# A decoder trunk's sparse-attention stage: two blocks of ties settled later, prompt jobs a slot deeper, row tiles scaled and rotated by GpSimd, loads reordered

## The reference

```
def _odd_layer(x, pos, mk, mv, attend, norm_g, w_in, qn, kn, w_out, mem_qn):
    xn = _rms(x, norm_g)
    q, k, v, g_c, qi, wi, ki, xq, g_x = _split(xn @ w_in, ODD_SPLITS)
    q = _rope(_rms(heads(q, AT_HEADS), qn), pos)      # 8 heads of 128
    k = _rope(_rms(heads(k, AT_KV_HEADS), kn), pos)   # 2 heads of 128
    yC = attend(q, k, v, qi, wi, ki).reshape(B, T, AT_W) * jax.nn.silu(g_c)
    y = jnp.concatenate([yC, yX.astype(yC.dtype)], axis=-1) @ w_out
    return x + y.astype(x.dtype), (k, v, ki)

def _index_select(qi, wi, ki, qpos, topk):
    s = ...                                           # indexer scores, -inf above the diagonal
    _, idx = lax.top_k(s, topk)                       # of equal scores the first ones
    return idx, idx <= qpos[None, :, None]

def _sparse_attend(q, kg, vg, valid):
    s = jnp.where(valid, einsum(q, kg) * Dh ** -0.5, -jnp.inf)
    return einsum(softmax(s), vg)
```

## Time and profile before

| what | value |
| --- | --- |
| median of 3 runs | 2043.4 us (2040.61 to 2052.66) |
| the profiled execution | 2048.12 us, of it the profile's span 2046.1 us |
| TensorE matmul busy | 1854.9 us, 91% |
| VectorE / ScalarE / GpSimd busy | 989.0 (48%) / 595.6 (29%) / 398.4 us (19%) |
| mean granted TensorE clock | 0.958 of full |
| back stage | 1576.7 to 2046.1, of it output products from 1886.0 |

### The profile page before, as it was taken

How to read it: one execution, slowest core, us unless ns; L and a number is a source line. 1 busy time by engine, 2 the same in 40 slices (tenths; PEclk the granted TensorE clock), 3 DMA queues, 4 the chain that set the end, 5 groups by cost and what they waited for, 6 DMA issues and landing times. The chain is left out here.

```text
span 2046.1 us, 26819 instructions
## 1 busy us (share of the span) xinstructions
PE 1854.9 (91%) x9553; PEld 1423.8 (70%) x9553; DVE 989.0 (48%) x2326; ACT 595.6 (29%) x1261; POOL 398.4 (19%) x639
## 2 busy tenths in 40 slices
PE   4999999999998997998999898999887897888998
PEld 3766788777787776886875466777665564666887
DVE  4522543224565645213431667778776555575211
ACT  1111332111111103101211347676534343444000
POOL 4201221000132342000331002211005515120000
PEclk9999999999899998998999998999988889899999
DMA  5334333544244547222122112324424834223221
GB/s 177 118 120 123 96 110 99 160 152 144 83 162 138 145 155 272 83 91 86 52 70 64 43 63 83 100 92 160 132 75 122 266 100 145 85 83 99 100 94 57
DMA packets 126950, 235.14 MB, mean 115 GB/s; under 512 B 28354, under 2 KB 52322, under 8 KB 126818
## 3 DMA queue, kind: packets, MB, share of 16 engines
q1 hardware_dynamic: 106706, 168.53, 25.5%
q0 software_dynamic: 18912, 60.57, 9.3%
q10 hardware_dynamic: 1200, 4.33, 0.5%
HBM read 167.22 MB, written 66.16 MB: 114 GB/s over the span
## 5 line engine op out<-in xcount | busy, mean ns | idle before, releaser
L1160 PE MATMUL layer_acc<-layer_w_hi,layer_xT_hi 128*128 128x512 f32 x640 | 266.2, 416 | 0.2 <-PE all_banks L1305 0.2
L1162 PE MATMUL layer_acc<-layer_w_hi,layer_xT_lo 128*128 128x512 f32 x640 | 256.5, 401 | 0.0
L1161 PE MATMUL layer_acc<-layer_w_lo,layer_xT_hi 128*128 128x512 f32 x640 | 256.3, 401 | 0.0
L2650 PE MATMUL front_acc<-front_w_hi,front_xT_hi 128*128 128x512 f32 x520 | 221.1, 425 | 15.9 <-DVE front_st L3104 8.2
L2652 PE MATMUL front_acc<-front_w_hi,front_xT_lo 128*128 128x512 f32 x520 | 208.3, 401 | 0.0
L2651 PE MATMUL front_acc<-front_w_lo,front_xT_hi 128*128 128x512 f32 x520 | 208.0, 400 | 0.0
L1160 PEld LDWEIGHTS layer_acc<-layer_w_hi,layer_xT_hi 128*128 128x128 f32 x640 | 124.4, 194 | 31.5 <-issue 6.1
L1161 PEld LDWEIGHTS layer_acc<-layer_w_lo,layer_xT_hi 128*128 128x128 f32 x640 | 123.7, 193 | 27.3 <-issue 2.6
L1162 PEld LDWEIGHTS layer_acc<-layer_w_hi,layer_xT_lo 128*128 128x128 f32 x640 | 123.2, 192 | 27.9
L2650 PEld LDWEIGHTS front_acc<-front_w_hi,front_xT_hi 128*128 128x128 f32 x520 | 100.3, 193 | 48.9 <-DVE front_st L3104 10.7
L2962 ACT ACTIVATE front_index_rows<-odd_bias,front_candidate 128x1024 bf16<-128x1024 f32 (+3 forms) x128 | 124.8, 982 | 6.9 <-DVEq L3285 5.0
(11 more groups left out here) (639 smaller groups left out, 3690.9 us busy)
## 6 DMA issues: line engine op xcount, KB each, us to landing
all_w<-in_w_even POOLq DMA_DIRECT2D x80, 256.0 KB, 3.9
h_even<-layer_st SPq DMA_DIRECT2D x79, 256.0 KB, 2.1
all_w<-in_w_odd POOLq DMA_DIRECT2D x61, 256.0 KB, 3.6
h_odd<-front_st SPq DMA_DIRECT2D x56, 256.0 KB, 2.0
layer_scratch<-h_even SPq DMA_DIRECT2D x51, 256.0 KB, 3.1
all_scratch<-in_w_mem SPq DMA_DIRECT2D x32, 256.0 KB, 3.7
back_first_smp<-in_cache_attn_v POOLq DMA_DIRECT2D x64, 128.0 KB, 3.2
all_scratch<-h_even SPq DMA_DIRECT2D x28, 256.0 KB, 3.7
```

The costliest lines, as they stand in the source:

```text
L1160: T.matmul(out[0:rows, :], xh[:, kk, to], wh[:, r, :], start=(kk == 0), stop=False)
L1161: T.matmul(out[0:rows, :], xh[:, kk, to], wl[:, r, :], start=False, stop=False)
L1162: ins = T.matmul(out[0:rows, :], xl[:, kk, to], wh[:, r, :], start=False, stop=(kk == KC - 1))
L2650: T.matmul(out[0:rows, :], xh[:, k, to], wh[:, r, :], start=(k == 0), stop=False, skip_group_check=True)
```

## The change

1. **Ties.** Blocks 5 and 4 leave the front stage; new streams `late_ties` (VectorE, slots 3, 5, 7, 9 of the back stage) and `late_biases` (ScalarE, slots 5 and 9) settle them, and job 32 waits for them. `find` is stepped once a slot in slots 62 to 71 (13 steps stood in 11 slots before), and `qk` starts at slot 62 instead of 63, with the transposes of its two tiles in two slots.
2. **Jobs.** The steps of a job are spread over four slots: mix of g-3, transposes of g-2, scores of g; three buffers `sm`, three `neg`, four `tot`. The plan has 77 slots.
3. **Row tiles.** `prep` starts at 8p-14. GpSimd now raises, multiplies by the root (L3769), by gamma (L3773) and rotates, each linked to the one before; VectorE keeps only the sums.
4. **Value pages.** GpSimd loads those of sequences 4 and 6, SyncE those of 5 and 7. SyncE loads row tile 2 ahead of the key pages of unit 3.
5. **Weights.** GpSimd starts the first four slices in slot 39, once the sample keys have been transposed; VectorE waits for the stored sample result instead.

```diff
-    for s, n in zip(range(62, 73), (2, 1, 1, 1, 2, 1, 1, 1, 2, 1, 1)):
-        plan[s] += ["find"] * n
+    for s in range(62, 72):
+        plan[s].append("find")
...
-    for s in range(63, 73):
+    for s in range(62, 73):
         plan[s].append("qk")
...
+    NOW = len(BY_DVE) + 1 + len(BY_ACT) - len(LATE_TIES)
...
-                todo = [(COL[i], P, rows_at(i)) for i in BY_DVE] + [(LAST, SMP, smp)] + [(COL[i], P, rows_at(i)) for i in BY_ACT]
+                todo = [(COL[i], P, rows_at(i)) for i in BY_DVE] + [(LAST, SMP, smp)] + [(COL[i], P, rows_at(i)) for i in BY_ACT if i not in LATE_TIES]
...
-            dve.wait_ge(nsd, NC)
+            dve.wait_ge(nsd, NOW)
...
+LATE_TIES = (5, 4)
...
-    for g in range(66):
+    for g in range(67):
         plan[g].append("job")
-    for s in range(41, 65):
+    for s in (3, 5, 7, 9):
+        plan[s].append("ties")
+    for s in range(39, 65):
         plan[s].append("weights")
-    for s in range(65, 76):
+    for s in range(66, 77):
         plan[s].append("out")
...
-    STEPS = [[(p, s - (8 * p - 15)) for p in range(2, T1) if 0 <= s - (8 * p - 15) < 6] for s in range(57)]
+    STEPS = [[(p, s - (8 * p - 14)) for p in range(2, T1) if 0 <= s - (8 * p - 14) < 6] for s in range(57)]
...
                 load_k(2)
+                load_qk(2)
                 load_k(3)
-                load_qk(2)
                 load_qk(3)
...
                         if step == 0:
                             pool.wait_ge(red, p - 1)
-                            G.tensor_tensor(ssq[u][0:rows, :], ssq[u][0:rows, :], c.half[0:rows, 0:H10], ALU.pow).then_inc(rsd, 1)
+                            link(G.tensor_tensor(ssq[u][0:rows, :], ssq[u][0:rows, :], c.half[0:rows, 0:H10], ALU.pow))
+                            link(G.tensor_tensor(y, y, bc(ssq[u][0:rows, :], 2, HD), ALU.mult))
                         if step == 1:
...
+                            for lo, hi, j, n in ((0, QH * HD, 0, QH), (QH * HD, QK, 1, KVH)):
+                                part = heads(qk[u][0:rows, lo:hi], n)
+                                link(G.tensor_tensor(part, part, bc(gam[0:rows, j, :], 1, n), ALU.mult))
+                        if step == 2:
+                            rotate(G, link, y, HD // 8, rt[:, PREP[p]], tmp, rows, H10)
+                            pool.sem_inc(rq, 1)
...
-                    if w in (4, 5, 8, 9):
-                        load_v(VRING + 2 * (w // 4 - 1) + w % 2, range(PAGES))
+                    if w in (4, 8):
+                        load_v(VRING + w // 4 - 1 + (w == 8), range(PAGES))
...
             def weights():
-                pool.wait_ge(sst, 16 * 2 * 4)
+                pool.wait_ge(ktr, 2 * (UNITS - 2))
...
-                    if g >= 2:
-                        mix(g - 2)
-                    if 1 <= g <= JOBS:
-                        transposes(g - 1)
+                    if g >= 3:
+                        mix(g - 3)
+                    if 2 <= g < JOBS + 2:
+                        transposes(g - 2)
                     if g < JOBS:
                         scores(g)
...
-                        if step == 1:
-                            dve.wait_ge(rsd, p - 1)
-                            V.tensor_tensor(y, y, bc(ssq[u][0:rows, :], 2, HD), ALU.mult).then_inc(scd, 1)
-                        if step == 2:
-                            dve.wait_ge(gd, 2 * (p - 1))
-                            rotate(V, link2, y, HD // 8, rt[:, t], tmp, rows, H10)
-                            dve.sem_inc(rq, 1)
...
+            def late_ties():
+                for i in LATE_TIES:
+                    j, w, v = 7 - i, P * (i + 1), c.bias[:, bias_at(i):bias_at(i + 1)]
+                    e, m, at = eq[:, 0:w], cum[:, 0:w], c.lowest[:, j:j + 1]
+                    link(V.tensor_scalar(e, v, at, 0.0, ALU.is_equal, ALU.add, accum_out=ties[:, :]))
+                    link(V.tensor_tensor_scan(m, e, e, 0.0, ALU.add, ALU.max))
+                    yield
...
```

More of the change, by code:

```diff
@@ L3475, in rotate @@
     link(eng.tensor_tensor(x2, t[2], t[3], ALU.add))
+LATE_TIES = (5, 4)
 def back_plan():
[L3480 removed]
+    plan = [[] for _ in range(77)]
     for s in range(1, 39):
@@ L3989, in outputs @@
                     yield
-            follow(plan, 0, None, prep=preps(), smp=smps(), job=jobs(), weights=idle(), out=outputs())
+            follow(plan, 0, None, prep=preps(), smp=smps(), job=jobs(), ties=idle(), weights=idle(), out=outputs())
         @block.scalar
```

128 lines of the change are left out of this document (81 added, 47 removed).

## The result

The changed kernel takes 2051.45 us, median of 20 runs, beside 2043.47 us for 20 runs of the kernel before: ratio 1.0037, 95% interval 1.0024 to 1.0050. It is 8 us slower by the medians, under the 1% that one measurement tells apart, but clear over so many runs.

What follows compares the result with a forecast made beforehand. TensorE was taken to bound the kernel, with row tile chains deciding its stalls. Terms -7.0, +15.2, -1.4 and +1.9 made +8.7 us on the median 2043.4, so 2052; bounds and the two near rivals reach 2027 and 2070.

Steps and rivals of the forecast that it cites:

- front stage: Front stage's end: without the ties of blocks 5 and 4 it comes 7.0 us earlier, between 3 and 10.
- back stage to slot 13: Back stage's start: GpSimd's 36 pages and two row tiles hold TensorE, +12.2 us, plus 3 for its clock: +15.2.
- slots 14 to 63: Back stage's later row tiles: windows of chain plus TensorE work, row tile 5 at +5.9, others mostly shorter: -1.4 us.
- end: After the last scores: one more slot of mixing and its reciprocal before the first output product, 6.0 becomes 8: +1.9 us.
- Late ties at nothing: Back stage slots 3 to 9: VectorE's some 9 us of ties lie under its waiting, so cost nothing; at most 9.
- Deeper jobs at nothing: Back stage slots: spreading jobs over more slots has little to win by itself; row tile chains decide.
- GpSimd's chain: Back stage row tiles: the chain takes 16.5 us, 18.5 with loads and contention, longer than its three slots in every block.
- clock term of +3: Back stage to slot 13: after a stall of about 10 us, some 3 us of TensorE work take twice their time.
- Weights and SyncE's pages at nothing: Back stage: SyncE's value pages and weights begun in slot 39 cost nothing, DMA being busy 0.2 to 0.5.
- contention rival: Back stage row tiles: contention stretches GpSimd's work, 2.3 us at each of seven tiles, giving 2068 us; chance 0.21.
- hidden chain: Back stage: ScalarE and GpSimd are ready long before TensorE, so the stalls go, giving 2007 us; chance 0.10.
- pages that run ahead: Back stage: GpSimd prepares pages while its tensor work runs, 20 of 36 save 0.6 us, giving 2033; chance 0.15.

Runs made afterwards that it cites:

- Experiment 1: Kernel before, with only the ties of blocks 5 and 4 moved into the back stage and the front's new plan: 2041.42 us, ratio 0.9979.
- version 10: Changed kernel, root product and rotation on VectorE, sequence 4's pages a slot later, ties back in the front stage: 2012.81 us, ratio 0.9851 to the kernel before.
- 8: Changed kernel, with root product and rotation back on VectorE and sequence 4's value pages a slot later: 2004.03 us, ratio 0.9821 to the kernel before.
- experiment 2: Kernel before, with only the jobs a slot deeper and three score buffers: 2025.73 us, ratio 0.9911.
- Experiment 7: Changed kernel, each row tile begun a slot earlier with its transposes left in place: 2033.36 us, ratio 0.9946 to the kernel before.
- experiment 3: Kernel before, with only the product with the root and the rotation moved to GpSimd, each linked: 2081.82 us, ratio 1.0191.
- experiment 4: Changed kernel, with the product with the root and the rotation back on VectorE: 2010.98 us, ratio 0.9829 to the kernel before.
- Experiment 5: Changed kernel, GpSimd's waits for its root and gamma products put off to where the result is used: 2037.9 us, ratio 0.9966 to the kernel before.
- experiment 6: Changed kernel, GpSimd's eight value pages of sequence 4 two slots later, behind row tile 5's rotation: 2047.47 us, ratio 1.0014 to the kernel before.

## Why the prediction came out, point by point

The time forecast was 2052, the measured one 2051.45. Stage by stage the terms are near too; but two parts of the change were priced far from their size, with opposite signs, and that these two errors are of one size was luck. The terms:

| term | forecast | in the profile |
| --- | --- | --- |
| front stage | -7.0 | -7.0 |
| back stage to slot 13 | +15.2 | +17.7 |
| slots 14 to 63 | -1.4 | -6.5 |
| end | +1.9 | +3.2 |
| sum | +8.7 | +7.4 |

**Front: right, by its own steps.** TensorE's waits of 1.44 and 1.29 went, the last product ended 2.8 us earlier in the stage (2.3 forecast), and the ties no longer held its end. Experiment 1 shows it alone (7.2).

**Late ties at nothing: wrong.** The step took VectorE's busy share (11.3 of 31.3 us) for cover. Experiment 1 showed 4.9 us of cost, 1.72 of it at a copy that TensorE waits for. In the changed kernel it can't be told from the rest; in version 10 against 8 it is 3.0.

**Deeper jobs at nothing: the largest error.** The prediction read 4.5 us of work in 5.1 of time in the earlier trace rows and then said that depth has little to win by itself. It never multiplied the 0.6 by the slots. In experiment 2 the whole back stage was 16.9 us shorter, ratio 0.9911; a slot of block 7 is 0.75 us shorter (in the changed kernel one of block 5 0.8). The formula for the windows hid the error: it took TensorE's busy time times clock for the new kernel, which leaves out just those waits, and the window's own length for the old one. So part of the gain was in the sum (-2.5, -4.1 and -1.0 in the last windows) without a name, while the text called it nothing.

**GpSimd's chain: the right mechanism, too small.** The prediction said that the chain of a row tile doesn't fit three slots, and that holds. From its squares to its transposes the chain took 13.9, 17.6 and 17.6 us at tiles 6 to 8, where 16.5 was forecast (18.5 without the 2 us ahead of the squares), and 1719.13 - 1695.24 = 23.9 at tile 5, where 23.7 was. The waits were 3.33, 5.73 and 6.11 at tiles 6 to 8, expected 3 to 5, and 14.42 at tile 5, expected about 10; tile 4, expected to wait too, did not. Experiment 7 shows that a slot more takes 2 to 6 us off each part from slot 18 on.

But the price of the move by itself was 39 us (experiment 3) and 42 when undone (experiment 4, 1.0037 to 0.9829), where my terms for it came to 22 (the expectation of experiment 3). Three things are in the difference. First, those 22 took 12 us for the start from the recorded sum, and that sum had already set off the earlier load of row tile 2 against GpSimd's work: GpSimd's wait for the first sums is 9.22 us in experiment 3 and 2.94 in the changed kernel, so 6.3 us of the 17 are an error of the 22 and not of the prediction. Second, the immediate waits. The prediction took 1.15 us for each page; behind a waited-for product three pages took 4.07 to 4.37 us and not 3.45, 3.1 us more in the four gaps. In the kernel before, pages behind GpSimd's work were issued at some 0.55 each, since their numbers had been read while it ran. I had this in a row (four issues in 2.25 us) and used it only for a rival. Experiment 5 shows the whole of it, some 2.4 us lost in each gap and 14 us in the time. Against it, the product over 1280 columns took 2.33 us and not 2.95; the 2.95 was scaled by columns from another product, so that it is twice VectorE's 1.49 showed nothing, and the measured ratio is 1.6. Third, the later parts: in experiment 3 slots 26-33 are 9.1 us longer, 42-49 3.4 and 50-63 5.0, where the terms had 6 at row tile 5 and 1 or less for the others. In the changed kernel itself GpSimd was through with its second tile 77.8 us into the stage, forecast 74.1. One wait of about 10 us was expected at the first or second tile; there were two, 7.29 and 10.46. The clock term of +3 is near: in the 4 us from 1598 the granted clock was 0.55 and in the 5 us from 1641 it was 0.50, which costs some 2 us at each (an estimate: half of the time at half clock).

One row was read for more than it says. The prediction put the 3.26 us at 1776.12 among the stalls around row tiles and held it to be no longer due with the weights of slot 39 in place. The transposes of row tiles waited 1.4 us in all before, so the chain did not decide then; and the same place in the changed kernel, slot 43, still shows most of it:

```profile
1775.84 2.90 PE L3958 MATMUL all_banks<-back_v,back_first_scratch 128*128 128x128 f32 x12 [2.36 <-issue]
```

**Value pages.** That SyncE takes half of them and that the eight of slot 27 lengthen tile 5's chain was right; experiment 6 took 10 us of that wait away. What their place is worth in the time is 3 to 5 us, not the 9 that I expected of experiment 6, because the pages then come late for the value products: two needs for one queue.

**Weights and SyncE's pages at nothing: open, and probably wrong.** Experiment 4's kernel is 34.9 us faster than before by its ratio, and the jobs (18.2) and ties (4.3) by themselves give 22.5. Some 12 us are left for the weights begun in slot 39, SyncE's value pages, the first row tile loaded sooner, the start at 8p-14, and for what these parts give only together. About half may be at the start: up to slot 13 it took 62.8 us with late ties, and experiment 1, with late ties alone, 68.8, while GpSimd's wait for the first sums fell from 9.88 to 2.47; that points at the earlier load. Slots 34-41 and 42-49 took 30.5 and 33.4 with all of them and 34.8 and 37.0 with the depth alone. None of them was tried alone, so which part gives what is not shown.

**The rivals.** The contention rival, my case for a slower kernel, did not come: the product with the root took 2.33 us at tiles 2 to 6 and 2.76 and 2.79 at tiles 7 and 8, where VectorE splits weights; rotations over all tiles averaged 3.35 us, for 3.05. That is some 0.5 us a tile, not 2.3. The Trainium skill, "SBUF — State Buffer", section "Who interferes with whom", has a VectorE instruction with two SBUF inputs contend with GpSimd's reads; the stretch beside the splits at tiles 7 and 8 agrees, and the whole is about a fifth of what I had given it. The hidden chain and the pages that run ahead did not come either, the latter for the reason given with it, the links, as experiment 5 confirms.

So the number was right and its story half right. The late start and the stalls at row tiles are there, near the size forecast for the whole; but the deeper jobs are worth 18 us and the move to GpSimd -39, and neither was seen at its size. Without the experiments the agreement would have passed for understanding.

## What to carry to other kernels

A wait that an engine makes right after its own instruction costs more than the wait: everything that its queue could have prepared meanwhile (reading a page number, issuing loads) is laid bare behind it. Put such waits where the result is used. And when one sum serves for a change of several parts, price each part by itself and let each be undone by itself; a sum that comes out can hide a part that should be taken back (here, leaving the row work on VectorE gives 2004 to 2011 us for 2051). A small wait in every slot of a long loop is worth more than a large one that occurs once: multiply before calling it nothing.

## What the runs showed of the hardware

- GpSimd's product of 1280 columns with one number a head took 2.33 us, one of 1024 columns with a row of gamma 2.36: the time did not go by the columns. Against VectorE's 1.49 us for the first that is 1.6 times. By the Trainium skill's factor of about two ("GPSIMD Engine Reference", section "4.1 Engine selection") it would be 3.0, an estimate; the measurement is lower, and it decides.
- A value page with a number read at run time takes GpSimd 1.15 us, of which 0.6 can lie under a running tensor instruction of its own (experiment 5: 0.54 to 0.61 a page behind a product); 1.2 us stand before the first page behind a waited-for instruction.
- The stages ahead of the touched ones have the same code in all fourteen kernels, and yet the front stage's first product stood anywhere from 945.6 to 956.9 us in their profiled executions. The front stage itself, in the ten kernels with late ties, took 612.1 to 613.0. So a difference of 5 us between two spans says nothing by itself; the length of a stage does.
